# Gate and up products of a SwiGLU chunk as a 2x2 block product with seven block products, in a four-layer fp32 trunk

## The reference, cut to what matters

```
D_MODEL = 1024;  D_FF = 2816
def half_ffn(x, i, n):
    h = 0.5 * ((silu(x @ w1[i, n]) * (x @ w3[i, n])) @ w2[i, n])
    return layer_norm(ALPHA * x + h, ln_g[i, 2 * n], ln_b[i, 2 * n])
```

## Time and profile before

| | us |
|---|---|
| median of 3 runs | 2655.02 (2654.42 to 2655.47) |
| the profiled execution, its own time | 2656.54 |
| its span, first to last instruction | 2654.8 |
| PE busy | 2575.1 (97%) |
| weight loads busy (beside PE) | 2300.9 (87%) |
| DVE busy | 1102.3 (42%) |
| ACT busy | 802.2 (30%) |
| POOL busy | 78.3 (3%) |
| granted TensorE clock, mean | 0.989 |

### The profile page before, as it was taken

How to read it: one execution, slowest core, us unless ns; L and a number is a source line. 1 busy time by engine, 2 the same in 40 slices (tenths; PEclk the granted TensorE clock), 3 DMA queues, 4 the chain that set the end, 5 groups by cost and what they waited for, 6 DMA issues and landing times. The chain is left out here.

```text
span 2654.8 us, 37436 instructions
## 1 busy us (share of the span) xinstructions
PE 2575.1 (97%) x16164; PEld 2300.9 (87%) x16164; DVE 1102.3 (42%) x1481; ACT 802.2 (30%) x1231; POOL 78.3 (3%) x169
## 2 busy tenths in 40 slices
PE   8999999979999999999999999999998999999998
PEld 8998998779989987899899887666665899899986
DVE  4223334553233336733233352555555733232267
ACT  3212221132122213522122223555555322122133
POOL 3000000100000000000000001000001000000000
PEclk9999999889999999999999999999999999999999
DMA  5213221322132222232132225666766332232121
GB/s 168 78 60 92 80 76 52 97 72 80 60 91 80 68 67 89 89 85 75 51 105 67 74 70 152 176 172 189 206 196 174 111 88 62 74 88 72 60 92 64
DMA packets 376612, 259.07 MB, mean 98 GB/s; under 512 B 10433, under 2 KB 339137, under 8 KB 376448
## 3 DMA queue, kind: packets, MB, share of 16 engines
q1 hardware_dynamic: 371344, 239.64, 31.1%
q0 software_dynamic: 5104, 17.04, 2.0%
HBM read 248.22 MB, written 8.42 MB: 97 GB/s over the span
## 5 line engine op out<-in xcount | busy, mean ns | idle before, releaser
L1642 PE MATMUL ps<-xt_hi,ring 128*128 128x384 f32 (+1 forms) x6144 | 1348.5, 310 | 34.4 <-DVE xt_lo L1346 16.5
L1642 PEld LDWEIGHTS ps<-xt_hi,ring 128*128 128x128 f32 x6144 | 1040.0, 190 | 49.1 <-issue 24.9
L1642 PE MATMUL ps<-xt_lo,ring 128*128 128x256 f32 (+1 forms) x3072 | 950.9, 310 | 0.0
L1642 PEld LDWEIGHTS ps<-xt_lo,ring 128*128 128x128 f32 x3072 | 584.9, 190 | 0.2
L1642 PE MATMUL ps<-ring,h_hi 128*128 128x512 f32 x1760 | 549.3, 392 | 0.0
L968 ACT ACTIVATE ring<-raw 128x1024 fp32r<-128x1024 f32 x326 | 324.6, 1029 | 443.8 <-PE ps L1642 351.5
L1278 DVE TENSOR_TENSOR ring<-raw,ring 128x1024 fp32r<-128x1024 f32 x326 | 381.5, 1198 | 144.9 <-ACT ring L968 140.5
L1642 PEld LDWEIGHTS ps<-ring,h_hi 128*128 128x128 f32 x1760 | 332.4, 189 | 68.8
L1528 DVE SCALAR_TENSOR_TENSOR act<-act,ps 128x384 f32<-128x384 f32 (+1 forms) x176 | 85.9, 488 | 678.7 <-PE ps L1642 678.7
L1642 PE MATMUL ps<-ring,h_lo 128*128 128x512 f32 x880 | 343.9, 391 | 0.0
L1177 ACT ACTIVATE h_hi<-act 128x384 fp32r<-128x384 f32 (+1 forms) x176 | 83.1, 472 | 636.7 <-DVE act L1528 636.7
(11 more groups left out here) (126 smaller groups left out, 1466.9 us busy)
## 6 DMA issues: line engine op xcount, KB each, us to landing
raw<-in_ffn_w_dram SPq DMA_DIRECT2D x256, 512.0 KB, 4.4
k_raw<-in_cache_k_dram SPq DMA_DIRECT2D x128, 256.0 KB, 5.3
v_raw<-in_cache_v_dram SPq DMA_DIRECT2D x128, 256.0 KB, 4.1
raw<-in_sb_w_in_dram SPq DMA_DIRECT2D x24, 512.0 KB, 6.2
raw<-in_ple_w_gate_dram SPq DMA_DIRECT2D x16, 512.0 KB, 4.6
g_b<-in_ln_g_dram POOLq DMA_DIRECT2D x8, 512.0 KB, 4.1
b_b<-in_ln_b_dram POOLq DMA_DIRECT2D x8, 512.0 KB, 5.4
raw<-in_ffn_w_dram SPq DMA_DIRECT2D x16, 256.0 KB, 3.5
```

Source lines behind the costliest of these rows:

```text
L1642: return pe.matmul(out, w, xx, start=first, stop=last, skip_group_check=True)
```

## The change: what it does, and the diff

The gate and the up product of a chunk are seen as one product of 2 x 2 blocks: the output has rows (gate, up) and columns (token half 1, token half 2; a half has 64 tokens of each tile, 320 in all), and the sum over the model's 1024 features has two halves of 512. In place of eight block products there are seven, on sums of blocks.

- **Weights.** The seven operands of 512 columns are: half blocks of gate and up, and four sums. POOL makes the sums, in `s1`, `s2` and in place in `raw` (`weight_sums`, `last_weight_sum`). ACT and DVE split seven items of 512 columns for a chunk, in place of two units of 1024.
- **Tokens.** Behind every head's turned tile, DVE makes four sums of 256 columns (`halves_low`), ACT five copies (`halves_hi`), DVE the lo parts of the plain blocks, POOL those of the sums (`sums_rest`; for the last tile DVE, `last_sums_rest`).
- **Products.** Each is 4 x 3 matmuls of 320 columns. The first four go to four PSUM banks, 4 to 6 are added to the banks of 0, 2 and 3, after what lay there has been read. DVE and ACT form gate and up from them. In the first chunk of a head, products 0 to 3 run for tiles 0 to 2 and then, after tile 4 is turned, for tiles 3 and 4.
- **Buffers.** The ring has 5 slots, and a slot holds two items. FFN features come in four parts of 5, 6, 5 and 6 chunks, each `gu` followed by its `down`. `raw` keeps three slots; a gate unit is released when item 5 is split, an up unit when item 6 is. ACT and DVE split item `n + 10` at the place of their programs where product `n` is dealt with (`ahead`).
- The pooling bands are built during the last `down` of the first FFN in place of the start. Some attention buffers lie elsewhere.

```diff
-RING = 7
+RING = 5
+HALVES = 2 * RING
+PARTS = ((0, 5), (5, 6), (11, 5), (16, 6))
+PRODUCTS = 7
+TH = TOKENS // 2
+TM = P // 2
+PIECES = (slice(0, 3), slice(3, TILES))
...
+        def ahead(n):
+            limit = n + 1
+            while limit < len(items) and all(b <= n for b in before[limit]):
+                limit += 1
+            return limit
...
         def raw_released(key):
-            return (pool_units[1] if key == "scale" else key) + 1
+            if key == "scale":
+                return item_of[pool_units[1]] + 1
+            st = stage_of_unit[key]
+            if st.kind == "gu":
+                k, up = divmod(key - st.u0, 2)
+                return item_of[st.quad0 + k, 6 if up else 5] + 1
+            return item_of[key] + 1
+        def source(n):
...
+            return (raw[:, gate, 0:HALF], s2[:, q % 2, :], s1[:, q % 2, :], raw[:, up, 0:HALF], raw[:, gate, HALF:],
+                    s2[:, q % 2, :], raw[:, up, HALF:])[j]
+        def source_ready(n):
...
+            if j in (0, 4, 6):
+                u = unit_of_quad[q] + (j == 6)
+                return w_loaded[raw_slot(u)], load_count[u]
+            return sums_done, 4 * q + {2: 1, 1: 2, 3: 3, 5: 4}[j]
...
+            def weight_sums(q):
...
+                pool.wait_ge(w_loaded[raw_slot(u)], load_count[u])
+                pool.wait_ge(w_loaded[raw_slot(u + 1)], load_count[u + 1])
+                if q >= 2:
+                    pool.wait_ge(w_split, item_of[q - 2, 5] + 1)
+                pool.tensor_tensor(s1[:, q % 2, :], up[:, 0:HALF], up[:, HALF:], ALU.add).then_inc(sums_done, 1)
+                pool.wait_ge(sums_done, 4 * q + 1)
+                pool.tensor_tensor(s2[:, q % 2, :], s1[:, q % 2, :], gate[:, 0:HALF], ALU.subtract).then_inc(sums_done, 1)
+                pool.tensor_tensor(up[:, 0:HALF], gate[:, 0:HALF], up[:, 0:HALF], ALU.subtract).then_inc(sums_done, 1)
+            def last_weight_sum(q):
...
+                pool.wait_ge(w_split, item_of[q, 1] + 1)
+                pool.wait_ge(sums_done, 4 * q + 2)
+                pool.tensor_tensor(s2[:, q % 2, :], raw[:, raw_slot(u), HALF:], s2[:, q % 2, :],
+                                   ALU.subtract).then_inc(sums_done, 1)
...
+                        weight_sums(q)
+                        if at_head:
+                            for t in range(2):
+                                sums_rest(st.prev, t)
+                        last_weight_sum(q)
+                        if at_head:
+                            for t in range(2, PROMPT_TILES):
+                                sums_rest(st.prev, t)
...
+            def halves_hi(st, t):
...
+                se.wait_ge(x_turned, g + 1)
+                if t >= 2:
+                    se.wait_ge(x_hi_done, 4 * (g - 1))
+                    se.wait_ge(t_lo_done, 8 * st.head0 + 2 * (t - 2) + 2)
+                se.activation(t_sum[:, t % 2, 3], x12, ACT.Copy).then_inc(x12_copied, 1)
+                se.activation(to_x1, x1, ACT.Copy).then_inc(x_hi_done, 1)
+                se.activation(to_x22, x22, ACT.Copy).then_inc(x_hi_done, 1)
+                se.wait_ge(t_done, 4 * g + 1)
+                se.activation(to_t1, t_sum[:, t % 2, 0], ACT.Copy).then_inc(x_hi_done, 1)
+                se.wait_ge(t_done, 4 * g + 4)
+                se.activation(to_more, t_sum[:, t % 2, 1:4], ACT.Copy).then_inc(x_hi_done, 1)
...
ACT, a chunk:
+                        for j in range(PRODUCTS):
+                            if j == 0:
+                                se.wait_ge(product_full, PRODUCTS * q + 1)
...
+                                se.activation(first_saved[:, :], ps[:, st.bank(q, 0), 0:TH], ACT.Copy).then_inc(first_copied, 1)
+                            if j == 4:
...
+                                se.activation(act[:, 0:TH], ps[:, st.bank(q, 0), 0:TH], ACT.Silu).then_inc(act_done, 1)
+                            if j == 5:
+                                se.wait_ge(gate_2_done, q + 1)
+                                se.activation(act[:, TH:], act[:, TH:], ACT.Silu).then_inc(act_done, 1)
+                            before_attention(st, ahead(item_of[q, j]))
+                        se.wait_ge(prod_done, 2 * q + 2)
+                        se.activation(in_halves(h_hi)[:, q - st.quad0], act_of_tiles, ACT.Copy).then_inc(h_hi_done, 1)
...
DVE, a chunk:
+                            if j == 1:
...
+                                ve.tensor_tensor(common[:, :], sums[1], first_saved[:, :], ALU.add).then_inc(common_done, 1)
+                            if j == 2:
...
+                                ve.tensor_tensor(up_2[:, :], sums[2], common[:, :], ALU.add).then_inc(shared_done, 1)
+                            if j == 3:
...
+                                ve.tensor_tensor(up_2[:, :], sums[3], up_2[:, :], ALU.add).then_inc(up_2_done, 1)
+                            if j == 5:
...
+                                ve.tensor_tensor(act[:, TH:], sums[2], common[:, :], ALU.add).then_inc(gate_2_done, 1)
+                            if j == 6:
...
+                                ve.tensor_tensor(common[:, :], sums[3], common[:, :], ALU.add).then_inc(up_1_done, 1)
...
+                                ve.scalar_tensor_tensor(act[:, TH:], act[:, TH:], 0.5, up_2[:, :], ALU.mult,
+                                                        ALU.mult).then_inc(prod_done, 1)
...
+                                ve.scalar_tensor_tensor(act[:, 0:TH], act[:, 0:TH], 0.5, common[:, :], ALU.mult,
+                                                        ALU.mult).then_inc(prod_done, 1)
+                            before_attention(st, ahead(item_of[q, j]))
+                        ve.wait_ge(h_hi_done, q + 1)
+                        ve.tensor_tensor(in_halves(h_lo)[:, q - st.quad0], act_of_tiles,
...
PE, a chunk:
+                        if st.head and q == st.quad0:
+                            turn_halves(prev, 3)
+                            for piece in range(2):
+                                if piece == 1:
+                                    turn_halves(prev, 4)
+                                    pe.wait_ge(t4_lo_done, 2 * prev.head0 + 2)
...
+                                for j in range(4):
+                                    ins = product(st, q, j, piece)
...
+                        else:
...
+                            for j in range(4):
+                                product(st, q, j).then_inc(product_full, 1)
+                        pe.wait_ge(first_copied, q + 1)
+                        product(st, q, 4).then_inc(product_full, 1)
+                        pe.wait_ge(shared_done, q + 1)
+                        product(st, q, 5).then_inc(product_full, 1)
+                        pe.wait_ge(up_2_done, q + 1)
+                        product(st, q, 6).then_inc(product_full, 1)
```

More of the change, by code:

```diff
@@ L107, with __init__, first, chunks @@
 class Stage:
-    def __init__(self, kind, layer, n=0, half=0, ln=None, then="none"):
-        self.kind, self.layer, self.n, self.half = kind, layer, n, half
+    def __init__(self, kind, layer, n=0, part=0, ln=None, then="none"):
+        self.kind, self.layer, self.n, self.part = kind, layer, n, part
         self.ln, self.then = ln, then
         self.head = False
-        self.part0 = self.y0 = self.gate0 = self.norm0 = self.piece0 = self.free0 = self.u0 = 0
+        self.y0 = self.gate0 = self.norm0 = self.piece0 = self.free0 = self.u0 = self.quad0 = self.head0 = 0
         self.prev = None
     @property
-    def per_dh(self):
[L120 to L130, removed]
+    def first(self):
+        return PARTS[self.part][0]
+    @property
+    def chunks(self):
+        return PARTS[self.part][1]
+    @property
+    def per_dh(self):
+        return {"down": (self.chunks + 1) // 2, "embed": 5, "out": 4, "v": 4}[self.kind]
+    @property
+    def counted(self):
+        return {"down": self.chunks // 2 if self.chunks % 2 else self.chunks // 2 - 1, "embed": 3, "out": 3, "v": 3}[self.kind]
     def piece_at(self, t):
         return self.piece0 + t + 1
+    def bank(self, quad, role):
+        k = quad - self.quad0
+        group = k % 2 if self.head else 1 - k % 2
+        if group:
+            return 4 + role
+        return role if self.prev.kind == "embed" else (role + 2) % 4
 def plan_stages():
-    stages = [Stage("load", 0, then="split")]
+    stages = [Stage("load", 0, then="halves")]
     for layer in range(DEPTH):
@@ L141, in plan_stages @@
         for n in range(2):
-            for half in range(2):
-                stages.append(Stage("gu", layer, n, half))
-                stages.append(Stage("down", layer, n, half))
+            for part in range(len(PARTS)):
+                stages.append(Stage("gu", layer, n, part))
+                stages.append(Stage("down", layer, n, part))
             stages[-1].ln = 2 * n
@@ L170, in plan_stages @@
             units += 2 * st.per_dh
-            free += 2 * {"down": 5, "out": 3, "embed": 3}[st.kind]
+            free += 2 * st.counted
```

(10 more changed lines are left out.)

637 lines of the change are left out of this document (393 added, 244 removed).

## The result

The changed kernel takes 2837.4 us (median of 4 runs, 2834.5 to 2848.8); the kernel before took 2655.2 beside it. The ratio is 1.069, interval 1.066 to 1.072: 7% slower, 12.6 us under the forecast of 2850. The profiled execution is the one of 2848.8 us (span 2846.8), the longest of the four by 10 us; its span is 192.0 us more than before.

What follows compares the result with a forecast made beforehand. PE's moved columns in the four FFNs were taken as the bound; 2656.5 - 155 + 196 + 48 + 99 + 11 = 2855.5 us profiled, 2854 for the median, stated as 2850, 7% slower; range 2650 to 2930.

Steps and rivals of the forecast that it cites:

- Seven products for eight: FFN chunks on PE: 84 matmuls of 320 columns at 0.147 us, 12.32 us for 14.08; -155 us over 88 chunks.
- The new loop: One raw slot's round per chunk: 15.8 us against PE's 12.32, so 3.5 us of wait, 56 times; +196 us.
- the six points: The links of the slot's round, from load to steps 1 and 2: sum 16.4 us, less overlaps 15.8.
- exclusion: POOL and a DVE operation with two SBUF inputs exclude each other; in the round DVE waits for POOL's third sum.
- First chunks of a part: Twelve parts that are no heads: product 5 can start 12.8 us after down, due after 8.8; +48 us.
- Heads: Four heads: later starts, first four products in two pieces, tile 4's chain unhidden, late next load; +99 us, bounds 55 and 130.
- Edges: Ends of parts before down's last chunk, 8 x 0.7 = +6 us, and last down of an FFN +5; +11 in all.
- The loop hides: Rival: load lands in 3.3 us, DVE splits beside POOL, loop 13.3 us, heads remain; 2662 us, chance 0.17 (loop 13.3 to 14.5).
- Faster, the ring's lead carries it: Rival: items split ten ahead, loop within PE's 12.32 us, only heads 80 and edges 20 cost; 2600 us, chance 0.18.
- The point at which it decides: Loop excess over PE's 12.32 us at which 56 excesses plus heads 80 and edges 20 equal 155: 1.0 us.
- The clock falls in the stalls: Rival: PE's clock drops in every chunk's waits, PE needs 16.4 us a chunk; 2880 to 2910 us, chance 0.07.

Runs made afterwards that it cites:

- r1: On the changed kernel, a chunk's last steps (h_hi, h_lo) go ahead of the splits of steps 5 and 6, on ACT and DVE: 2752.3 us.
- r2: On the changed kernel, the gate slot is given back after item 4's split and the fourth sum, not after item 5's split: 2774.0 us.
- r3: On the changed kernel, POOL's third and fourth weight sums cover 256 of 512 columns, half of each left out: 2776.9 us.
- r4: On the changed kernel, the edits of r1 and r2 together: 2700.9 us.
- r12: On r11, at a non-head part's first chunk DVE makes both first sums ahead of the splits that need POOL's sums: 2632.0 us, ratio 0.993.
- r7: On r4, r6's head edits, plus ACT saving the first product ahead of its splits and DVE splitting one step later: 2655.3 us, ratio 1.001.
- r10: On r7, the first four products at a head run over 320 columns at once instead of 192 and 128: 2642.2 us, ratio 0.996.
- r11: On r7, the edits of r9 and r10 together: 2645.7 us, ratio 0.998.
- r9: On r7, the last splits of the down stage stop at the next part's item (1, 0): 2656.9 us.
- r6: On r4, four reorderings at the heads alone, among them turning tile 4 inside the first piece: 2680.8 us.

## Why the prediction was right

The sum was made against the profiled execution and gave 2855.5; the profiled execution of after took 2848.8, the highest of its four runs. The mechanism, a loop through one `raw` slot that is longer than PE's work, was right. That the sum came within 7 us is luck: the loop's term was 43 us too high, and the heads (11), the first chunks (4) and the edges (21) together 36 too low. The median of the runs, for which 2854 was worked out, is 17 below that. By the steps:

**Seven products for eight.** Right: 320 columns go every 0.147 us, though the blocks are read in runs of 64 columns:
```profile
205.87 0.46 PE L1938 MATMUL ps<-xt_hi,ring 128*128 128x320 f32 x2
206.17 0.31 PE L1938 MATMUL ps<-xt_lo,ring 128*128 128x320 f32 x1
206.31 0.46 PE L1938 MATMUL ps<-xt_hi,ring 128*128 128x320 f32 x2
```
**The new loop.** Its mechanism was right link by link; r1, r2 and r3 each shortened one link, and the turn became 1.37, 1.07 and 0.9 us shorter. By the six points, in the rows of the round above:

| point | predicted | measured | from |
|---|---|---|---|
| 1 load | 4.0 | 4.35 | 202.50 to 206.85 |
| 2 two sums | 2.9 | 2.70 | to 209.55 |
| 3 hi, lo, exclusion | 2.1 | 1.76 | to 211.31 |
| 4 step 6 | 2.5 | 2.13 | to 213.44 |
| 5 `h_hi`, copy, hi, lo | 2.5 | 2.25 | to 215.69 |
| 6 steps 1 and 2 | 2.4 | 2.08 | to 217.77 |

Sum 15.3 against 16.4, less 0.6 of overlaps that the measured points already hold. The largest part of the error is POOL's, some 0.4 us: 1.29 us for 512 columns where the line from the earlier trace rows gave 1.39; the load took 0.35 more than put. This round is a little longer than the median turn of 15.05, by which the term is 56 x 2.73 = 153 for 196.

**First chunks of a part.** 52 us for 48, as what remains beside the rounds.

**Heads.** 110 for 99, by errors that cancel in part. The second piece was put at 4.5 us "or more if a small matmul has a floor". It took 10.3 (43.97 to 54.27): at the full clock its 48 matmuls would take 5.4 (0.112 each), and the rest is the lower clock behind the 5.0 us of idle. Over the four head stages the lower clock costs 44 us where it cost 7 before, so it is up to a third of the 110. The chain of tile 4 was put at 6.6 with its transposes and took 6.1 (37.91 to 43.97). The first product at the start came at 30.2, as forecast, and the pooling's 9.7 later in place of 11, but embedding and attention output came 14.7 and 10.1 later in place of 12 and 7:
```profile
30.16 0.50 PE L1938 MATMUL ps<-xt_hi,ring 128*128 128x192 f32 x1 [13.47 <-POOL x_lo L1065]
...
43.97 0.47 PE L1938 MATMUL ps<-xt_hi,ring 128*128 128x128 f32 x1 [5.02 <-DVE x_lo L1610]
...
608.14 0.50 PE L1938 MATMUL ps<-xt_hi,ring 128*128 128x192 f32 x1 [6.89 <-issue]
```
The last row answers to the earlier trace rows.

**Edges.** The term that was put far too low: 32 us for 11. At each of eight ends of a part PE waits 1.86 us for `h_lo` in place of 0.7, since the ring split of step 6 ahead of it was held back like the others; r4, where `h_lo` stands ahead of the splits, has 0.27 in its place. That is 15 of the 32; of the rest 7 lie in four `down` stages that ran at a granted clock of 0.96, 3.5 at the start of the `v` stage and 4 at the end of the kernel, not taken apart; some 3 are not placed.

**Rivals.** "The loop hides" gave 2662: wrong, the turn is 15.05 us and the exclusion is there (r3). "Faster, the ring's lead carries it": wrong as a forecast for this code, but r12 shows that the lead was long enough and the order of the queues spent it. The point at which it decides, a turn of 13.3 us, was itself off: r4, with a turn of 12.89, is still 49 us above before, since heads and edges cost more than the 80 + 20 of that sum, and the first chunks, which it leaves out, cost too. r12, with a turn of 12.77 and shorter heads and first chunks, came out under the kernel before. "The clock falls in the stalls": at heads, and in few of the rounds (ten episodes of 3.4 us in all `gu` stages). By the granted clock over PE's busy time (the time ahead of the clock's first entry counted at the lower level) the lower level costs 28 us before and 93 after, 44 of them in the head stages and 14 in the other `gu` stages. PE's idle times over 0.15 us are 69 and 300 us. How much of the 65 us more lies beside other engines' work was not tried.

## What to carry to other kernels

A saving on the bound engine counts only if the helpers' work fits by order, not by busy share: follow one buffer slot round (freed, loaded, prepared, consumed, freed), add up also what stands ahead of each step in its engine's queue, and hold the sum against the bound engine's time per turn. If it is longer, look first for an instruction whose data have long been ready and which stands behind one that waits; of the 205 us between the changed kernel and r12 some 145 came from such moves alone (r1, r7, r12), 51 from an earlier release (r4) and 10 from wider matmuls (r10, r11), and none needed memory. Check the same sum again after each fix, with the place in the queue and not the time at which data are ready: that was the mistake in r1 and r9.

## What the runs showed of the hardware

- GpSimd and VectorE hold each other up in both directions. Where VectorE is seldom idle, GpSimd's sums of 512 columns take up to 1.88 us in place of 1.29 (r1, at 212.25), and a multiplication of 0.48 on VectorE becomes 1.60 (r1, at 209.53).
- GpSimd needs 0.456, 0.741, 1.29 and 1.85 us for 128, 256, 512 and 768 columns of such sums: a line of 2.2 ns a column and 0.17.
- A matmul of 128 or of 192 columns costs 0.213 us at the lower clock level (granted clock 0.50; after, r7) and 0.112 or 0.111 at the full one (r6, r7). One of 320 costs 0.147 at the full one, also where it reads runs of 64 columns.
- Behind 5.0 us of idle PE the matmuls kept the lower level's spacing for 15 us (after, 43.97 to 58.92), behind 2.4 us for 14 (r7, 33.78 to 47.55), though PE was busy throughout. Behind a wait of 1.8 us it was at the lower level for 3.4 us (after, 216.0 to 219.4), and behind most waits of the rounds not at all.
